# Stick-breaking heads with queries on partitions: reversed scans, and TensorE turning scans and scores by unit matrices

## The reference

```python
def stick_breaking_attention(q, k, v):
    ...
        z = jnp.einsum('bhtd,bhsd->bhts', q[:, :, t0:t1], k[:, :, :t1]).astype(jnp.float32) * scale
        valid = (s_pos < t_pos) & (s_pos >= LEAD_PAD)
        log_beta = jax.nn.log_sigmoid(z)
        log_keep = jnp.where(valid, jax.nn.log_sigmoid(-z), 0.0)
        log_tail = lax.cumsum(log_keep, axis=3, reverse=True) - log_keep
        w = jnp.where(valid, jnp.exp(log_beta + log_tail), 0.0)
        outs.append(jnp.einsum('bhts,bhsd->bhtd', w.astype(v.dtype), v[:, :, :t1]))
```

## Time and profile before

| | us |
|---|---|
| median of 3 runs | 1741.87 (1740.36 to 1744.36) |
| the profiled execution, its own time | 1742.63 |
| its span in the trace | 1740.9 |
| mixing stage in it, from the first scores to the output product | 1028.0 to 1187.2 |
| busy over the span: PE, DVE, ACT, POOL | 1607.4, 819.9, 335.7, 238.3 |
| mean granted TensorE clock | 0.976 |

### The profile page before, as it was taken

How to read it: one execution, slowest core, us unless ns; L and a number is a source line. 1 busy time by engine, 2 the same in 40 slices (tenths; PEclk the granted TensorE clock), 3 DMA queues, 4 the chain that set the end, 5 groups by cost and what they waited for, 6 DMA issues and landing times.

```text
span 1740.9 us, 19130 instructions
## 1 busy us (share of the span) xinstructions
PE 1607.4 (92%) x7778; PEld 1030.6 (59%) x7778; DVE 819.9 (47%) x1360; ACT 335.7 (19%) x574; POOL 238.3 (14%) x298
## 2 busy tenths in 40 slices
PE   7999999999999896878599988999999998999996
PEld 5688888886888432333488875778643333333332
DVE  7898645536464511111743249985532322332233
ACT  3422000027100210100311154651201010000011
POOL 1100003200000310110200005781120000000000
PEclk9999999999999998999799999999999999999998
DMA  5122222220237999999422200015899999999993
GB/s 203 49 97 97 73 97 97 98 73 25 76 146 284 305 407 409 425 428 414 190 98 73 97 25 1 1 44 220 327 378 430 429 429 429 429 430 430 430 430 143
DMA packets 54080, 403.27 MB, mean 232 GB/s; under 512 B 13776, under 2 KB 15184, under 8 KB 25952
## 3 DMA queue, kind: packets, MB, share of 16 engines
q1 hardware_dynamic: 46560, 389.34, 55.6%
q0 software_dynamic: 7424, 12.61, 2.0%
HBM read 397.69 MB, written 16.81 MB: 238 GB/s over the span
## 4 chain that ended last, share of the span: by engine, by line
PE 72%; DMA 14%; DVE 5%; ACT 2%; issue 2%; POOL 2%; SPq 2%; POOLq 0%; DVEq 0%; ACTq 0%
PE bank L1751 38%; PE bank L738 13%; PE bank L753 6%; DMA arena<-in_expert_in 4%; PE bank L717 2%; DMA arena<-in_expert_gate 2%; DMA ring<-in_expert_up 2%; DMA arena<-in_expert_up 2%; DMA ring<-in_expert_gate 2%; DMA arena<-in_expert_out 2%; DMA ring<-in_expert_in 1%; PE bank L1743 1%; PE bank L718 1%; PE bank L920 1%; PE bank L1862 1%
## 5 line engine op out<-in xcount | busy, mean ns | idle before, releaser
L738 PE MATMUL bank<-arena 128*64 128x512 f32 x960 | 273.8, 613 | 30.1 <-DMA arena<-in_expert_in 12.3
L738 PE MATMUL bank<-ring,arena 128*64 128x512 f32 x576 | 184.1, 618 | 9.9 <-issue 5.4
L738 PEld LDWEIGHTS bank<-arena 128*64 128x64 f32 x960 | 84.0, 140 | 174.9 <-issue 173.9
L1127 DVE TENSOR_TENSOR resid<-resid,bank 128x512 f32<-128x512 f32 x120 | 80.7, 685 | 202.9 <-PE bank L718 202.9
L2435 DVE CAST ring_high<-ring 128x2048 fp32r<-128x2048 f32 x51 | 63.0, 1236 | 238.3 <-DMA ring<-in_stream_a 147.4
L2436 DVE TENSOR_TENSOR ring_low<-ring,ring_high 128x2048 fp32r<-128x2048 f32 x60 | 138.7, 2312 | 6.4 <-ACT ring_high L2107 4.5
L753 PE MATMUL bank<-arena 128*64 128x512 f32 x448 | 114.4, 595 | 14.3 <-DVE arena L1153 7.2
L1751 PE MATMUL bank<-ring_low,xn_high 128*128 128x512 f32 x288 | 113.1, 393 | 0.3 <-DVE ring_low L2436 0.3
L1751 PE MATMUL bank<-ring_high,xn_high 128*128 128x512 f32 x288 | 112.3, 390 | 0.0
L1751 PE MATMUL bank<-ring_high,xn_low 128*128 128x512 f32 x288 | 112.2, 390 | 0.0
L738 PEld LDWEIGHTS bank<-ring,arena 128*64 128x64 f32 x576 | 55.9, 141 | 70.6 <-issue 70.6
(11 more groups left out here) (395 smaller groups left out, 3067.2 us busy)
## 6 DMA issues: line engine op xcount, KB each, us to landing
ring<-in_stream_a SPq DMA_DIRECT2D x42, 1024.0 KB, 5.1
arena<-in_expert_gate SPq DMA_DIRECT2D x20, 2048.0 KB, 23.7
arena<-in_expert_in SPq DMA_DIRECT2D x18, 2048.0 KB, 27.6
arena<-in_expert_up SPq DMA_DIRECT2D x18, 2048.0 KB, 24.6
arena<-in_expert_down SPq DMA_DIRECT2D x18, 2048.0 KB, 25.1
ring<-in_expert_up SPq DMA_DIRECT2D x12, 2048.0 KB, 25.7
ring<-in_expert_down SPq DMA_DIRECT2D x12, 2048.0 KB, 25.4
ring<-in_expert_gate SPq DMA_DIRECT2D x12, 2048.0 KB, 25.3
```

The lines of the kernel that those rows point to most:

```text
L738: last = nc.tensor.matmul(h[side * SLOTS:(side + 1) * SLOTS, :], tokens[:, k, side * SLOTS:(side + 1) * SLOTS], w[:, k * 512:(k + 1) * 512 ...
L1127: nc.vector.tensor_tensor(place, place, bank[bank_at][:, :], ALU.add).then_inc(m.moe_added, 1)
```

## The change

The scores of a head now have the queries on partitions and the keys along the row. The first 512 columns are the four diagonal blocks, then come the "rests" of the four query blocks: 16, 144, 272 and 400 keys that lie before the diagonal block (16 meta keys and whole blocks), 1344 columns in all. Padding keys are no longer computed. VectorE copies, scales and masks the diagonal blocks; ScalarE copies and scales the rests. The sums along the keys are eight reversed scans on VectorE (`tensor_tensor_scan` over `part[:, ::-1]`), which add max(z, 0), a Relu that ScalarE writes to `above_zero`, and the logarithm in the same instruction; each rest begins with the first column of its diagonal scan. TensorE then computes, for each of ten blocks and four meta blocks, scores x unit matrix minus scans x unit matrix in PSUM: that turns the block, so that keys stand on partitions, and subtracts. ScalarE takes the exponential out of PSUM into `w_turned` (ring 1). VectorE's subtractions and logits and GpSimd's block sums go.

The order of the turn changes: turned units 0 and 1 stand behind the step of place 1, units 2 and 3 behind that of place 2, and the head's output ahead of the step of place 3 of the same turn, so there are nine turns. ScalarE computes the weights at place 2. VectorE's scans stand at place 2, in turn 0 ahead of the first state products. The row norms move up by a turn (`head_square` place 0, `head_sums` place 1, `head_norm` place 2). In turn 8 two more `mT` units are turned early, and one with `mT` 6. The load of the last weight tile's first half (ring 1) and everything behind it on SyncE waits for the last head's output. The value product's meta piece has 16 rows instead of 128. GpSimd writes the negative unit matrix once, near the start of the program.

```diff
-    put("strict", np.where(row < col, 0.0, NEG))
+    put("strict", np.where(col < row, 0.0, NEG))
...
-TURNS = SBH + 2
+TURNS = SBH + 1
...
-        zw = [at(arena, i * STICK, [STICK]) for i in range(3)]
+        zw = [at(arena, i * STICK, [STICK]) for i in (2, 3)]
+        above_zero = at(arena, STICK, [STICK])
+        w_turned = at(ring[1], 0, [TURNED])
...
-                    sp.wait_ge(psum_filled2, U2.filled(("R", SBH - 2, NT2 - 1)))
+                    sp.wait_ge(psum_filled2, U2.filled(("WT", SBH - 2, 3)))
+                if n == first + 2 * len(STREAM2) - 2:
+                    sp.wait_ge(psum_filled2, U2.filled(("SO", SBH - 1)))
...
             def scores(h):
...
+                b = begin2(("Z", h, 0))
+                for t in range(NT):
+                    last_ = product(b[:, t * P:(t + 1) * P], t, sbk[half, h // 2, (t + 1) * P:(t + 2) * P])
+                end2(last_)
+                for j in (1, 2):
+                    b = begin2(("Z", h, j))
+                    for t in SCORE_UNITS[j]:
+                        a = REST_AT[t] - REST_AT[SCORE_UNITS[j][0]]
+                        last_ = product(b[:, a:a + REST_W[t]], t, sbk[half, h // 2, PAD:PAD + REST_W[t]])
+                    end2(last_)
+
+            def exponents_turned(g, units):
                 pe.wait_ge(sums_ready, g + 1)
...
+                def turned(out_, a, w):
+                    nc.tensor.matmul(out_, zw[g % 2][:, a:a + w], c("ident"), start=True, stop=False)
+                    return nc.tensor.matmul(out_, sps[g % 2][:, a:a + w], minus_ident[:, :], start=False, stop=True)
+
+                for j in units:
+                    b = begin2(("WT", g, j))
+                    if j < 3:
+                        for n, (s, t) in enumerate(TURNED_UNITS[j]):
+                            last_ = turned(b[:, n * P:(n + 1) * P], t * P if s == t else REST_AT[t] + META + s * P, P)
+                    else:
+                        for t in range(NT):
+                            last_ = turned(b[0:META, t * P:(t + 1) * P], REST_AT[t], META)
                     end2(last_)
 
             def stick_out(g):
-                pe.wait_ge(weight_ready, g + 1)
+                wait_read2(pe, ("WT", g, 3))
...
+                    if place == 3 and i >= 1:
+                        stick_out(i - 1)
                     if step_after(i, place) is not None:
                         step(step_after(i, place))
+                    if place in (1, 2) and i >= 1:
+                        exponents_turned(i - 1, (0, 1) if place == 1 else (2, 3))
...
+            def stick_scores(h):
+                if h >= 2:
+                    act.wait_ge(psum_filled2, U2.filled(("WT", h - 2, 3)))
+                for j in (1, 2):
+                    b, ts = unit2(("Z", h, j)), SCORE_UNITS[j]
+                    a, end = REST_AT[ts[0]], REST_AT[ts[-1]] + REST_W[ts[-1]]
+                    read2(A.activation(zw[h % 2][:, a:end], b[:, 0:end - a], ACT.Copy, scale=SBD ** -0.5))
...
             def stick_log(h):
                 v = sps[h % 2]
+                if h >= 1:
+                    act.wait_ge(sums_ready, h)
+                A.activation(above_zero, zw[h % 2], ACT.Relu).then_inc(log_ready, 1)
                 act.wait_ge(act_step, 2 * h + 2)
                 A.activation(v, v, ACT.Ln, bias=1.0).then_inc(log_ready, 1)
 
             def stick_weights(g):
-                wait_read2(act, ("R", g, NT2 - 1))
-                A.activation(zw[g % 3], zw[g % 3], ACT.Exp).then_inc(weight_ready, 1)
+                for j, unit in enumerate(TURNED_UNITS):
+                    b, w = unit2(("WT", g, j)), P * len(unit)
+                    read2(A.activation(w_turned[:, SEQ * j:SEQ * j + w], b[:, 0:w], ACT.Exp))
+                b = unit2(("WT", g, 3))
+                read2(A.activation(w_turned[0:META, META_AT:META_AT + SEQ], b[0:META, :], ACT.Exp))
...
+            def sums_from_last(v, a, w, initial):
+
+                part = v[:, a:a + w][:, ::-1]
+                return V.tensor_tensor_scan(part, part, above_zero[:, a:a + w][:, ::-1], initial, ALU.add, ALU.add)
+
+            def stick_sums(h):
+                v = sps[h % 2]
+                dve.wait_ge(log_ready, 2 * h + 2)
+                for t in range(NT):
+                    ins = sums_from_last(v, t * P, P, 0.0)
+                then(ins)
+                for t in range(NT):
+                    ins = sums_from_last(v, REST_AT[t], REST_W[t], v[:, t * P:t * P + 1])
+                ins.then_inc(sums_ready, 1)
...
+                    if place == 2 and i < SBH:
+                        stick_sums(i)
+                    if place == 1 and i >= 2:
+                        head_sums(i - 2)
...
+            G.tensor_scalar(minus_ident[:, :], c("ident"), -1.0, None, ALU.mult).then_inc(ids_ready, 1)
```

More of the change, by code:

```diff
@@ L233, in first_block_units @@
     return u
[L238 to L241, removed]
+REST_W = [META + t * P for t in range(NT)]
+REST_AT = [SEQ + sum(REST_W[:t]) for t in range(NT)]
+STICK = SEQ + sum(REST_W)
+SCORE_UNITS = ((), (0, 1, 2), (3,))
+TURNED = 10 * P + SEQ
+TURNED_UNITS = (((0, 0), (0, 1), (0, 2), (0, 3)), ((1, 1), (1, 2), (1, 3), (3, 3)), ((2, 2), (2, 3)))
+TURNED_AT = {at: SEQ * n + P * j for n, unit in enumerate(TURNED_UNITS) for j, at in enumerate(unit)}
+META_AT = 10 * P
 STICK_BANKS, STATE_BANKS = (0, 1, 2, 3, 4), (5, 6, 7)
@@ L280, in norm_orders @@
                     sums.append(("state", h - 1))
-            if place == 3 and 2 <= i < SBH + 1:
+            if place == 0 and i >= 2:
                 squares.append(("stick", i - 2))
@@ L284, in norm_orders @@
                 sums.append(("state", HGH - 1))
-            if place == 1 and 3 <= i < SBH + 2:
-                sums.append(("stick", i - 3))
+            if place == 1 and i >= 2:
+                sums.append(("stick", i - 2))
     return squares, sums
@@ L303, in normed_order @@
                 rows.append(("state", n // LEVELS - 1))
-            if place == 2 and i >= 3:
-                rows.append(("stick", i - 3))
+            if place == 2 and i >= 2:
+                rows.append(("stick", i - 2))
     return rows
@@ L354, in second_block_units @@
             if place == 0 and i < SBH:
[L355 to L362, removed]
+                for j in range(3):
+                    u.add(("Z", i, j), "act" if j else "dve", STICK_BANKS)
+            if place == 3 and i >= 1:
+                u.add(("SO", i - 1), "act", STICK_BANKS)
             n = step_after(i, place)
@@ L365, in second_block_units @@
                 step(n)
+            if place in (1, 2) and i >= 1:
+                for j in (0, 1) if place == 1 else (2, 3):
+                    u.add(("WT", i - 1, j), "act", STICK_BANKS)
             if (i, place) == (SBH, 0):
@@ L369, in second_block_units @@
                 u.add(("HO", HGH - 1), "act_state", STATE_BANKS)
-    for k in TURN_ORDER[3:]:
+                for k in (0, 1):
+                    u.add(("mT", k), "dve", LATE_BANKS)
+            if (i, place) == (SBH, 2):
+                for k in (2, 6):
+                    u.add(("mT", k), "dve", LATE_BANKS)
+    for k in (7, 3):
         u.add(("mT", k), "dve", LATE_BANKS)
@@ L1753, in half_product, with tile_product @@
                 return ins
-            def tile_product(n, pieces, left, right, begin, end, ready=None, behind=None):
+            def tile_product(n, pieces, left, right, begin, end, ready=None, behind=None, rows=lambda i: P):
                 units = [key for key, _, _ in pieces]
@@ L1974, in _ @@
             columns2_with_meta("sbk")
[L1975 removed]
+            rows2("sbv", hT_parts, with_meta=True)
             columns2("hq")
@@ L2272, in _ @@
             for t in range(NT2):
-                b = unit2(("sbv", t))
-                read2(A.copy(sbv[:, t, :], b[:, :]))
+                b, rows = unit2(("sbv", t)), P if t else META
+                read2(A.copy(sbv[0:rows, t, :], b[0:rows, :]))
             for m_ in range(4):
@@ L2355, in _ @@
                         level_exp(n + 1)
-                    if place == 0 and 2 <= i < SBH + 1:
-                        stick_weights(i - 2)
                     if place == 0 and i < SBH:
+                        stick_scores(i)
                         stick_exp(i)
```

151 lines of the change are left out of this document (55 added, 96 removed).

## The result

The kernel after takes 1792.62 us (1791.29 to 1798.62) against 1743.11 for the kernel before on the same chip. The ratio on record is 1.0274, interval 1.0247 to 1.0301; the two medians by themselves give 1.0284. The forecast was 1745.8 with a range up to 1756. So the sign of the likeliest case was right and its size wrong by a factor of thirteen: +49.5 us instead of +3.9.

A forecast was written before the change was run, and what follows sets the result against it. The prediction took TensorE to bound the stage: +3.3 us at the start, +0.5 in turns 2 to 7 and +0.1 at the end gave +3.9, moving the median from 1741.87 to 1745.8, with a range of 1736 to 1756.

The forecast's parts named there:

- The step that failed: Stick-breaking stage: TensorE near full length from turn 3 on, priced at 1.68 ns a column and 0.22 us a product.
- The new wait: TensorE ahead of each head's output: idle until ScalarE has exponentiated the last turned unit, priced at 0.9 us a turn.
- Output: Head's output product on TensorE: again 14 products, 3.1 us, unchanged by the 16-row meta blocks.
- Turned units: TensorE products replacing the sums: 28 products of 128 columns, 6.2 us a turn, +1.05 against the sums before.
- Scores: TensorE's score products of a head: 1328 columns plus the 16-column one, 2.45 us, so -0.75 a turn.
- The end: From the last level to the output product: 17.6 us against 17.5 before, +0.1.
- The start: Turns 0 and 1: first scans delay the first turning to 1046.3; turn 2 starts 3.3 us later.
- Scans: VectorE's eight reversed scans over 1344 columns: 3.6 us a head, between ends of 1.8 and 5.6.
- Relu over 1344 columns: ScalarE's new pass, 1.3 us; on VectorE, by the skill's bf16 figure, the sum would be 0.9 less, once.
- A: Rival at turned unit 3 to output: wait under 0.3 us a turn, relief worth more, -3.0 us, 1738.9; chance 0.28.
- B: Rival: the loop ScalarE, scans, level products becomes the bound if scans exceed 5.5 us; +13 us, 1755; chance 0.20.
- C: Rival: moved work is hidden by TensorE and turn 1 catches up the late start; 0 +- 2 us, 1742; chance 0.10.

The follow-up runs named there:

- full_fill_start: Changed kernel with 128-row meta products, four unread products filling the wait before each output, and the first head's scans in turn 1: 1747.32 us, 1.0034.
- start_warm: full_fill_start plus 28 and 20 unread products in the two long idle stretches of turn 1: 1744.18 us, 1.0027 of the kernel before.
- full_fill: Changed kernel with 128-row meta products in the head's output and four unread products filling the wait before it: 1752.32 us, 1.0068.
- after_order_full: Changed kernel with place 3's step issued ahead of the head's output and the meta products over all 128 rows: 1762.95 us, 1.0109.
- before_gap: Kernel before, with the exponential of a head's last 512 columns issued late, so TensorE idles ahead of each output: 1783.23 us, 1.0244.
- before_warm: Kernel before, with 20 unread products ahead of the first turning of state keys and 24 ahead of the first block sums: 1738.78 us, 1.0010.

## Why the prediction was wrong

**The step that failed** is the one under the whole sum: "from turn 3 on TensorE is at or near its full length in each window", and from there all its terms at 1.68 ns a column and 0.22 a product. These are prices at full clock. The clock column stood in the earlier trace rows, 1.00 in turns 2 to 8 and 0.79 in the first two, and the forecast used it for turn 1 alone. It didn't ask whether the change itself would take it down, though it put an idle stretch and the thinnest products of the kernel (16 rows, 64 columns) at the same spot of every turn. No rival held it either.

**The new wait** was found, placed and sized rightly: "idle 0.7 to 1 us ahead of the head's output", measured 0.68. The groups of the kernel after, 1020 to 1270:
```profile
L2026 PE MATMUL bank<-arena,ring 128*128 128x64 f32 x160 | 30.3, 332 | 4.7 <-ACT ring L2346 4.7
...
L2028 PE MATMUL bank<-arena,ring 16*128 16x64 f32 x64 | 16.3, 341 | 0.0
...
L2337 ACT ACTIVATE arena<-arena 128x1344 f32<-128x1344 f32 x8 | 10.5, 1309 | 0.0
L2346 ACT ACTIVATE ring<-bank 16x512 f32<-16x512 f32 x8 | 4.7, 586 | 11.0 <-PE bank L2007 11.0
```
Seven waits cost 4.7 us, and the last exponential 0.59. The price of what follows the wait was not in the row.

**Output: "again 14 products, 3.1".** 4.1 at full clock with the 16-row blocks, 3.07 with 128 rows. The product of 16 rows was priced by its columns.

**Turned units, 6.2 forecast:** 6.4 in full_fill_start (3.57 from 1063.81 and 2.84 from 1068.27). **Scores, 2.45:** 2.69. **Wait, 0.9:** 0.88 in its place with the filling products (1071.11 to 1071.99). A level right behind the scores or the output takes 0.95 to 1.04 us instead of 0.89, about 0.2 a turn. Together some 0.6 a turn too low. Turns 2 to 6 of start_warm take 97.5 us (its windows above) where the forecast had 5 x 16.3 + 12.0 = 93.5: 3.0 of the 4.0 are these, and two waits of 0.2 for VectorE are part of the rest.

**The end, +0.1.** Turns 7 and 8 of start_warm take 35.5 us, where the forecast had 16.3 + 17.6 = 33.9. The first two turnings take 1.6 with a wait of 0.54 between them, instead of 0.9, and the filling products add 0.9 ahead of the last output, where two turnings already stand. The other two waits were in the sum: 0.77 of 0.8 forecast, and 1.59 (for VectorE's low part) within the 2.3 from output to product, measured 2.2. The 4.0 and the 1.6 are the 133.0 - 127.4 = 5.6 us that turns 2 to 8 take beyond the forecast at full clock.

**The start, +3.3.** The first turning was forecast at 1046.3, 18.3 behind the first scores; in full_fill it comes 18.1 behind them (1041.46 after 1023.35), as in the kernel after (1042.42 after 1024.32). That part held. From there to turn 2 the forecast had 17.4 us, full_fill takes 21.25, at half clock until 1051; so the start came to 39.4 - 32.4 = 7.0. With the scans moved (full_fill_start) it is 2.7, with the clock up as well (start_warm) 0.3.

**Scans, 3.6 a head:** 3.7 for head 0 in the kernel after, 3.9 to 4.1 for heads 1 to 6 and 5.4 for head 7. A scan of 400 columns takes 1.02 to 1.26 us, where the pace taken from the 128-column scan gives 0.91. Reading in reverse costs nothing that can be seen: four reversed scans of 128 columns take 1.38 in a row, 0.35 each, against 0.34 forward. Relu over 1344 columns took 1.31, as forecast for a pass of that width, and none of TensorE's waits in turns 2 to 8 ends with it. No run put it on VectorE, so the 0.9 that the forecast would take off for that is not shown; the figure it was worked out from is for bf16, and this pass is fp32.

**The rivals.** A fell: the wait is 0.68. B did not happen in the change as made (scans at 3.7 to 4.1 in turns 0 to 6, one wait of 0.2 for a level product), but its chain appeared when the order was changed (after_order_full). C fell.

**How the 52.7 us add up, roughly.** Turns 2 to 8 take 169.3 in the kernel after and 133.0 in start_warm, 36.3 more. By the clock of their windows 67 us of the 169.3 were at half clock, 34 lost; 16-row blocks cost 7 x 1.06, 7. That is 41, an upper bound, since half clock under a wait loses nothing. The remaining 16.4 of the 52.7 are the 6.2 by which those turns are longer than before at full clock (133.0 against 126.8) and 10.3 in turns 0 and 1 (42.7 against 32.4), which hold the late start and 26 us at half clock, partly idle. What the runs show is that the clock and the rows carry it; the split to the microsecond is arithmetic.

## What to carry to other kernels

Where a stage runs at a granted clock of 1.00, ask of each change what it puts right behind dense work: here a short wait and thin products in one place halved the clock for up to 17 us, and TensorE's prices in them doubled. The cheap mend here was more work, not less: zero rows up to 128, and products that nobody reads in the wait. Try it on the place that recurs in every turn; a single stretch at the start was worth nothing that could be measured in either kernel.

## What the runs showed of the hardware that was not expected

- Between products of 128 rows a 16-row product isn't cheaper, but dearer: 0.36 against 0.22 us a block of 64 columns at full clock, and the block behind it is late too. What a series of 16-row products would cost, no run shows.
- In the kernel after the two work together. At half clock stand 98.9 us with both, 37.5 without the wait, 27.3 without the narrow rows and 20.5 without either, the last all in the start. The kernel before shows 13.7 with neither and 51.2 with 32 rows; its waits of before_gap are longer than 0.68, so 71.7 there is not the wait's share in the kernel after. No run here tells what exactly makes the clock fall.
- In the kernel after the fall comes late and stays: in turn 3 the wait ends at 1113.3, the clock falls at about 1116.3, and the dense turned units that come at 1129.5 run at full clock from their second pair on. In before_gap's turn 2 it falls within the wait of 3.8 us, ahead of the output (granted 0.80 at 1072 to 1073, 0.50 from then on).
- Taking away one stretch at half clock can make another (before_warm, 0.79 in turn 3).
